# A two-layer hybrid decoder trunk: the low parts of rotated keys and queries and of the recurrent output are computed on GpSimd instead of VectorE

## The reference

```python
h = rmsnorm(x, g)
z = h @ w_in        # u_lru, g_lru, q, g_nsa, kc, vc, ks, vs, kwn, vwn, gate_logits
y_lru = rg_lru(causal_depthwise_conv(u_lru, conv_w, conv_b), wa, ba, wi, bi, lam)
o_cmp, p_cmp = cmp_attention(q, compress(kc, ...), compress(vc, ...))
q_rot = apply_rope(q, cos, sin)
o_slc = slc_attention(q_rot, apply_rope(ks, cos, sin), vs, idx, ok)
o_win = win_attention(q_rot, apply_rope(kwn, cos, sin), vwn)
y_nsa = gates[0] * o_cmp + gates[1] * o_slc + gates[2] * o_win
y = concat([y_lru * silu(g_lru), y_nsa * silu(g_nsa)])
return x + y @ w_out
```

## Time and profile before

| | |
|---|---|
| median of 3 runs | 614.97 us (614.49 to 615.18) |
| the profiled execution | 615.78 us, of which the span from first to last instruction is 614.0 us |
| granted TensorE clock | 0.994 of full speed |
| TensorE busy | 577.4 us (94%) |
| VectorE busy | 402.7 us (66%) |
| ScalarE busy | 294.0 us (48%) |
| GpSimd busy | 40.6 us (7%) |
| the chain of waits that ended last | PE 63%, DVE 18%, ACT 9%, issue 6%, DMA 3%, POOL 1% |

### The profile page before, as it was taken

How to read it: one execution, slowest core, us unless ns; L and a number is a source line. 1 busy time by engine, 2 the same in 40 slices (tenths; PEclk the granted TensorE clock), 3 DMA queues, 4 the chain that set the end, 5 groups by cost and what they waited for, 6 DMA issues and landing times.

```text
span 614.0 us, 8688 instructions
## 1 busy us (share of the span) xinstructions
PE 577.4 (94%) x3207; PEld 405.2 (66%) x3207; DVE 402.7 (66%) x690; ACT 294.0 (48%) x586; POOL 40.6 (7%) x80
## 2 busy tenths in 40 slices
PE   4999999989989999999999999999999999999985
PEld 3777767777556555556887786777766666555664
DVE  4786976887454775755667498589755666565541
ACT  3647653624454554542533765363445445444521
POOL 1001101120000000000420110112000000000000
PEclk9999999999999999999999999999999999999997
DMA  8756394444111110101323838535311220000112
GB/s 246 198 158 166 85 216 111 86 104 128 35 36 35 35 28 9 36 0 37 102 71 108 216 87 193 133 74 115 92 47 36 68 61 10 1 2 1 35 34 69
DMA packets 94121, 50.71 MB, mean 83 GB/s; under 512 B 42992, under 2 KB 92288, under 8 KB 94080
## 3 DMA queue, kind: packets, MB, share of 16 engines
q1 hardware_dynamic: 91456, 45.95, 29.8%
q0 software_dynamic: 1536, 3.15, 2.1%
q10 hardware_dynamic: 1088, 1.06, 0.6%
HBM read 44.90 MB, written 2.10 MB: 77 GB/s over the span
## 4 chain that ended last, share of the span: by engine, by line
PE 63%; DVE 18%; ACT 9%; issue 6%; DMA 3%; POOL 1%; POOLq 0%; DVEq 0%; ACTq 0%
PE z_ps L1352 10%; PE z_ps L1354 8%; PE z_ps L1353 8%; PE s_ps L1411 6%; PE t_ps L1427 5%; PE a_ps L1463 4%; PE o_ps L1463 4%; ACT probs L929 3%; DVE w_lo L984 2%; DMA swp<-E 2%; PE o_ps L1352 2%; PE o_ps L1354 2%; PE o_ps L1353 2%; PE s_ps L1414 2%; DVE mn L1260 2%
## 5 line engine op out<-in xcount | busy, mean ns | idle before, releaser
L1352 PE MATMUL z_ps<-h_hi,w_hi 128*128 128x512 f32 x264 | 111.1, 421 | 3.1 <-DVE h_lo L977 2.3
L929 ACT ACTIVATE probs<-s_ps,mn 128x128 f32<-128x128 f32 (+3 forms) x128 | 66.3, 523 | 96.7 <-DVE mn L1260 87.9
L1354 PE MATMUL z_ps<-h_hi,w_lo 128*128 128x512 f32 x264 | 103.8, 393 | 0.0
L1353 PE MATMUL z_ps<-h_lo,w_hi 128*128 128x512 f32 x264 | 103.6, 393 | 0.0
L786 ACT ACTIVATE w_hi<-stage 128x1024 fp32r<-128x1024 f32 x58 | 61.1, 1055 | 73.7 <-PE z_ps L1354 44.6
L1260 DVE TENSOR_REDUCE mn<-s_ps 128x1 f32<-128x128 f32 (+3 forms) x128 | 56.8, 485 | 52.8 <-PE s_ps L1414 52.6
L984 DVE TENSOR_TENSOR w_lo<-stage,w_hi 128x1024 fp32r<-128x1024 f32 x58 | 71.0, 1224 | 10.5 <-ACT w_hi L786 9.3
L1352 PEld LDWEIGHTS z_ps<-h_hi,w_hi 128*128 128x128 f32 x264 | 49.9, 189 | 21.6 <-issue 13.7
L1354 PEld LDWEIGHTS z_ps<-h_hi,w_lo 128*128 128x128 f32 x264 | 49.8, 189 | 11.0
L1353 PEld LDWEIGHTS z_ps<-h_lo,w_hi 128*128 128x128 f32 x264 | 50.1, 190 | 7.8 <-issue 0.2
L1411 PE MATMUL s_ps<-k_st,q_st 64*128 64x128 f32 (+3 forms) x384 | 46.8, 349 | 5.1 <-ACT probs L929 5.0
(11 more groups left out here) (221 smaller groups left out, 913.6 us busy)
## 6 DMA issues: line engine op xcount, KB each, us to landing
stage<-in_w_in SPq DMA_DIRECT2D x28, 512.0 KB, 4.2
stage<-in_w_in SPq DMA_DIRECT2D x32, 256.0 KB, 3.8
stage<-in_cmp_k_w SPq DMA_DIRECT2D x8, 512.0 KB, 3.8
stage<-in_cmp_v_w SPq DMA_DIRECT2D x8, 512.0 KB, 4.9
stage<-in_w_out SPq DMA_DIRECT2D x8, 512.0 KB, 3.5
stage<-in_w_out SPq DMA_DIRECT2D x16, 256.0 KB, 3.8
swp<-E POOLq DMA_DIRECT2D x48, 64.0 KB, 2.0
out<-xT SPq DMA_DIRECT2D x8, 256.0 KB, 2.7
```

What stands on the lines that cost most here:

```text
L929: act.activation(probs[:, 4 * (u % 2) + j, 0:W], s_ps[g][:, 0:W], ACT.Exp, scale=-1.0, bias=mn[:, u % 2, j:j + 1], accum_out=rs[:, b, col: ...
L1352: pe.matmul(bank, w_hi[:, slot, at:at + P], x_hi, start=first, stop=False)
L1353: pe.matmul(bank, w_hi[:, slot, at:at + P], x_lo, start=False, stop=False)
L1354: ins = pe.matmul(bank, w_lo[:, slot, at:at + P], x_hi, start=False, stop=last)
```

## The change

The two step kinds LOW (rotated keys and queries) and YL for the recurrent tiles leave VectorE's part and stand in GpSimd's, at the same places of the list, with the same waits and the same semaphores. That is 6 LOW and 4 YL a layer, 20 instructions in all. The YL of the attention output (`st[2] == "n"`) stays on VectorE.

```diff
@@ block.gpsimd @@
+                elif kind == "YL" and st[2] != "n":
+                    _, l, t = st
+                    pool.wait_ge(ylru_hi, CT * l + t + 1)
+                    pool.tensor_tensor(y_lo[:, t, :], UC[t % 2], y_hi[:, t, :].bitcast(F32), ALU.subtract).then_inc(ylru_lo, 1)
+                elif kind == "LOW":
+                    _, l, name = st
+                    n, e = rope_no[(l, name)], e_slot((l, name))
+                    pool.wait_ge(rope_hi, n + 1)
+                    if stem(name) == "q":
+                        hi, lo = q_st[:, int(name[-1]), :], q_st[:, GROUP + int(name[-1]), :]
+                    else:
+                        hi, lo = (k_st[:, 0 if name == "ks" else 1, part, :] for part in range(2))
+                    ins = pool.tensor_tensor(lo, e, hi.bitcast(F32), ALU.subtract)
+                    ins.then_inc(rope_lo, 1)
@@ block.vector @@
-                elif kind == "YL":
-                    _, l, t = st
-                    dve.wait_ge(ylru_hi, CT * l + t + 1)
-                    dve.tensor_tensor(y_lo[:, t, :], UC[t % 2], y_hi[:, t, :].bitcast(F32), ALU.subtract).then_inc(ylru_lo, 1)
-                elif kind == "LOW":
-                    ...
-                    dve.wait_ge(rope_hi, n + 1)
-                    ...
-                    ins = dve.tensor_tensor(lo, e, hi.bitcast(F32), ALU.subtract)
-                    ins.then_inc(rope_lo, 1)
```

More of the change, by code:

```diff
@@ L1220, in _ @@
                     dve.tensor_tensor(e, e, turned, ALU.add).then_inc(rot_ok, 1)
-                elif kind == "LOW":
-                    _, l, name = st
-                    n, e = rope_no[(l, name)], e_slot((l, name))
-                    dve.wait_ge(rope_hi, n + 1)
[L1226 to L1229, removed]
-                    ins = dve.tensor_tensor(lo, e, hi.bitcast(F32), ALU.subtract)
-                    ins.then_inc(rope_lo, 1)
                 elif kind == "GAFF":
```

## The result

The changed kernel takes 632.1 us (median of 4 runs, 631.4 to 633.6) against 614.8 for the kernel before on the same chip: a ratio of 1.0271, interval 1.0247 to 1.0295. It is slower by 17.3 us. I had forecast 618.3 and at most 623.0. The direction was right, and the size is five times the forecast's.

A forecast was written before the change was run, and what follows sets the result against it. TensorE, busy 94%, bounds the kernel, so moves count only where it waits for VectorE. Losses 1.6 + 1.1 + 0.15 + 0.45 = +3.3 us on 614.97 gave 618.3 us, range 614.2 to 623.0.

The forecast's parts named there:

- GpSimd gets in when that ends: Tile 2, layer 0: LOW ks starts after `w_lo` and holds GM 1's first product by 0.92 us; priced +0.8.
- VectorE is never held: Rival for all moved pieces: GpSimd waits instead of VectorE, so the change wins time; 612.2 us, chance 12%.
- a running row keeps GpSimd out: Rival: back-to-back VectorE instructions block GpSimd until a gap, so LOW ks costs nothing; +2.1 us, 617.1, chance 20%.
- Tile 2, +1.6 and +1.1: Recurrent tile 2, layers 0 and 1: net loss from LOW ks, YL 0, LOW kw and YL 1, as TensorE waiting.
- The piece, 1.09 us: Each moved subtraction on GpSimd: assumed 1.09 us, like the undisturbed adding of squares, with 1.65 as upper end.
- float32r write: Rival: writing float32r makes GpSimd's piece 1.65 us, lengthening ten holds by 0.56 each; 625.7 us, chance 13%.
- YL 2, YL 3 and LOW q2 fall where VectorE waits for a swap: Query stretch, both layers: these pieces leave VectorE where it idles for a swap; that cover is short in layer 1.
- No SWAP is late: Query stretch: each SWAP stands ahead of its stretch's pieces, and the piece before is over by then; no loss.
- LOW q1, +0.15: Queries, each layer: leaving saves 0.75 us, but GpSimd then holds the gating product 0.92; net +0.15 at q3's CMP.
- Behind SWAP q3 in layer 1, +0.3: Two GpSimd pieces start the rotation 0.5 us later, delaying the transposed gates; 0.3 lost, bounds 0 and 0.65.

The follow-up runs named there:

- tile-2 half alone: The changed kernel with only LOW ks, LOW kw, YL 0 and YL 1 on GpSimd, the query pieces back on VectorE: 622.1 us, 1.0107 against the kernel before.
- late-low-parts kernel: The kernel before, all on VectorE, with LOW ks, LOW kw and YL 1 behind CONV 2 and LOW q1 behind SWAP q3: 617.0 us, 1.0025.
- kernel with the load held back: The changed kernel, with SyncE issuing the weight load behind the SWAP of q1, q2 and q3 only once that swap has landed: 625.0 us, 1.0151.
- waits filled: The changed kernel with unread matrix products put where TensorE waits, at tile 2, the q1 to q3 compressed-key products and the gates: 628.9 us, 1.0224.
- beside a fill: The changed kernel with each of GpSimd's 20 subtractions replaced by a zero fill of the same tile, which reads nothing: 624.3 us, 1.0146.
- at chosen times: The changed kernel with YL 0 back on VectorE, most other GpSimd pieces timed for expected VectorE slack, and loads held back: 615.6 us, 1.0001 against the kernel before.
- kernel with the fills: The kernel before, with GpSimd filling a spare tile behind SWAP q1, q2 and q3, one short fill in layer 0, three long in layer 1: 620.1 us, 1.0070.

## Why the prediction was wrong in size

- **Direction, and who is held: right.** "GpSimd gets in when that ends" held at the three places of tile 2 where a piece met a running row of VectorE instructions, so *VectorE is never held* and *a running row keeps GpSimd out* are both out.
- **Tile 2, +1.6 and +1.1: the mechanism right, the size partly by luck.** The waits grew by 1.3 and 1.4 us, 2.7 together as forecast, by the holds named. But in layer 0 VectorE's chain grew by 2.0 us, not 1.6: from the rotation of ks to CONV 2 it is 23.96 us before (59.01 to 82.97) and 25.95 after (58.26 to 84.21). The wait shows less of it because this execution entered the stretch 0.75 us earlier, and because TensorE itself lost time there, waiting 0.35 and 0.58 us for a weight load (82.37 and 83.58). With the tile-2 half alone the waits grew by 1.6 and 1.6.
- **The piece, 1.09 us: too small.** 1.27 to 1.32 undisturbed, and holds of 1.0 to 1.1 instead of 0.92. In size it is the *float32r write* rival in weak form, worth some 0.4 us at each layer's tile 2. Whether the type written is the reason, no run shows. It was not the cause of the miss.
- **"YL 2, YL 3 and LOW q2 fall where VectorE waits for a swap", "No SWAP is late": this is the step that failed.** The stages of the queries lost 5.9 us in waits (1.6 + 1.1 + 1.7 + 1.5) against a forecast of 0.6, and every swap of q1 to q3 ended late (last packet after 4.0 to 4.7 us instead of 3.0 to 3.7). I had priced what the pieces do on GpSimd and left out what their leaving starts: YL 2, LOW q1 and YL 3 stood directly in front of `w_lo`, `w_lo` frees the slot for the next load, and the load came 0.7 us earlier and met the swap. Holding the load back took away 7 of the 17 us (the waits left over those of the kernel before are 4.9 us in all, 2.6 at tile 2 and 2.3 at the queries, and two stretches at half clock 3.4), and in the late-low-parts kernel the same collision arose with no piece on GpSimd. That the two kinds of packets compete is what these runs show; in which part of the transfer path they do is open.
- **LOW q1, +0.15: too small.** I let GpSimd wait for the scan to end and hold the gating product by 0.92. It did not wait: it went in under the running scan, and the scan lost 1.58; the gating product kept its 0.69. Net 0.8 instead of 0.15 a layer, as the kernel with the load held back shows.
- **Behind SWAP q3 in layer 1, +0.3: too small.** The same kernel shows 0.75 there, with pieces of 1.30 instead of 1.09 us, above the bound of 0.65.
- **The clock: the second step that failed, a term put at nothing without a reason.** The prediction had no term for it, though the forecast itself lengthened a wait of 1.66 us to 3.3, in an engine that hardly stands elsewhere. In the offsets it makes up the other half of the loss, 8.0 us. With the waits filled, only some 3 us came back, so how much the clock costs by itself in this kernel lies between the two and stays open. The tile-2 half alone gives the cleanest figure: 3.2 us of waits cost 6.7 us.

The Trainium skill (page "SBUF — State Buffer", section "Who interferes with whom") says that a VectorE instruction with two SBUF inputs contends with a GpSimd instruction that reads SBUF and not with one that only writes. The runs agree: `w_lo` took 2.33 us beside a subtraction (75.65) and 1.22 beside a fill, the scan 2.81 and 1.23. It also says that an instruction with at most one SBUF input doesn't contend, outside the two-port modes; the 96-column instruction above, held to 1.28 us, was not told apart from such a mode here.

## What to carry to other kernels

Before an instruction is taken off an engine's list, look at what stands behind it and which transfer that releases: an engine that gets lighter starts transfers earlier, into others that had the path to themselves. In this kernel, moving a subtraction to GpSimd won VectorE 0.60 us and held it by 1.0 to 1.6 where it met an instruction that reads two inputs from SBUF, so it could pay only where VectorE is really idle; even at chosen times it brought nothing. Moving it later in VectorE's own list paid, 0.5%, with the load held back. Where a nearly always busy TensorE is made to wait some 2 us or more, count the clock behind the wait as a term of its own, with a price from nothing to 1.7 us (once 3.4) a wait.

## What the runs showed of the hardware

- A scan that was 0.4 us under way was stretched from 1.23 to 2.81 us by a GpSimd subtraction of 1.32 us. A `w_lo` that was 0.1 us under way was not: it kept its 1.23 us, and the piece waited (61.03, 2.27 us).
- Four transfers of 64 KB between SBUF partitions (q1) were over 2.98 us after the first issue when the next weight load (2 times 256 KB) was issued at 1.8 us; with the load at 1.03 to 1.06 us the six swaps of the kernel after took 4.0 to 4.7, and with the load at 1.4 to 1.5 us, in the kernel with the fills, 3.9 to 4.0. The signal was slower too: from the last packet to a rotation that waited for it 0.47 us before (q1), 1.0 to 1.2 after.
- The traces of all fourteen kernels have 28 waits of TensorE for VectorE of 1.88 to 3.28 us between 80 and 450 us. Behind 16 of them TensorE was granted 1.2 GHz within 2 us, for 3.4 us (once 6.8); behind 12 it wasn't, the longest of these 2.89 us. Behind none of the waits of 1.45 to 1.85 us in these stretches did it fall. The length of the wait alone doesn't tell which.
